# Mamba mixer of a one-core encoder step: step sizes with tokens on partitions, sample state products four at a time, and additions split around a convolution

## What is computed

```
def mamba2_mixer(u, conv_buf, ssm_state, w_in, conv_w, conv_b, dt_bias, A_log, Dp, norm_g, w_out):
    zxbcdt = u @ w_in
    ...
    xbc, new_buf = causal_conv(xbc, conv_buf, conv_w, conv_b)
    xbc = jax.nn.silu(xbc)
    ...
    dt = jax.nn.softplus(dt_raw.astype(jnp.float32) + dt_bias.astype(jnp.float32))
    A = -jnp.exp(A_log.astype(jnp.float32))
    y, s_new = ssd_scan(xs, dt, A, Bm, Cm, ssm_state)
    ...
    y = rmsnorm(y * jax.nn.silu(z), norm_g)
    return y @ w_out, new_buf, s_new
```

## Time and profile before

| | us |
|---|---|
| median of 3 runs | 1870.8 (1869.88 to 1873.21) |
| the profiled execution | 1868.97 |
| its span | 1867.2 |
| TensorE busy in it | 1822.4 (98%) |
| DVE busy | 1139.9 (61%) |
| ACT busy | 825.5 (44%) |
| POOL busy | 253.0 (14%) |

### The profile page before, as it was taken

How to read it: one execution, slowest core, us unless ns; L and a number is a source line. 1 busy time by engine, 2 the same in 40 slices (tenths; PEclk the granted TensorE clock), 3 DMA queues, 4 the chain that set the end, 5 groups by cost and what they waited for, 6 DMA issues and landing times.

```text
span 1867.2 us, 28243 instructions
## 1 busy us (share of the span) xinstructions
PE 1822.4 (98%) x10554; PEld 1735.5 (93%) x10554; DVE 1139.9 (61%) x1697; ACT 825.5 (44%) x1421; POOL 253.0 (14%) x299
## 2 busy tenths in 40 slices
PE   8999999999999999999999999999998999999997
PEld 8999999798888999999999999986777899999997
DVE  6545447888789754544775454456777756545444
ACT  5333325564574433333563333346665544333232
POOL 1000110313214000011400001122112130000110
PEclk9999999999999999999999999999999999999999
DMA  6444444465452534444444434441124534344441
GB/s 208 124 124 132 139 136 147 143 214 190 160 192 85 189 117 131 127 144 136 117 142 122 134 119 142 138 161 39 46 84 140 163 114 138 118 135 124 141 141 57
DMA packets 67652, 249.71 MB, mean 134 GB/s; under 512 B 8328, under 2 KB 9608, under 8 KB 66288
## 3 DMA queue, kind: packets, MB, share of 16 engines
q1 hardware_dynamic: 57584, 205.32, 36.0%
q0 software_dynamic: 9984, 43.24, 7.1%
HBM read 235.74 MB, written 12.12 MB: 133 GB/s over the span
## 4 chain that ended last, share of the span: by engine, by line
PE 79%; DVE 12%; ACT 4%; issue 2%; DMA 2%; POOL 1%; SPq 0%; DVEq 0%; POOLq 0%; ACTq 0%
PE pair L1854 23%; PE pair L1856 22%; PE pair L1855 22%; DVE wlo L1226 2%; PE pair L2273 1%; PE pair L2274 1%; PE pair L2275 1%; DVE cy L1354 1%; DMA lowA<-in_cacheT 1%; PE pair L2364 1%; ACT seg L842 1%; PE pair L2055 1%; DMA wv<-in_wv 1%; DVE xl L1236 1%; DVE S L1450 1%
## 5 line engine op out<-in xcount | busy, mean ns | idle before, releaser
L1854 PE MATMUL pair<-xh,whi 128*128 128x384 f32 x1928 | 651.3, 338 | 6.0 <-DVE xl L1236 4.9
L1856 PE MATMUL pair<-xh,wlo 128*128 128x384 f32 x1928 | 645.6, 335 | 0.0
L1855 PE MATMUL pair<-xl,whi 128*128 128x384 f32 x1928 | 645.5, 335 | 0.0
L1226 DVE TENSOR_TENSOR wlo<-raw,whi 128x1024 fp32r<-128x1024 f32 (+3 forms) x372 | 465.7, 1254 | 174.8 <-ACT whi L713 165.7
L713 ACT ACTIVATE whi<-raw 128x1024 fp32r<-128x1024 f32 (+2 forms) x369 | 378.6, 1029 | 283.1 <-PE pair L1856 269.9
L1854 PEld LDWEIGHTS pair<-xh,whi 128*128 128x128 f32 x1928 | 362.9, 188 | 15.0 <-issue 9.1
L1855 PEld LDWEIGHTS pair<-xl,whi 128*128 128x128 f32 x1928 | 362.9, 188 | 1.7 <-issue 1.0
L1856 PEld LDWEIGHTS pair<-xh,wlo 128*128 128x128 f32 x1928 | 362.7, 188 | 0.0
L1246 DVE TENSOR_TENSOR tg<-pair,rstd 128x384 f32<-128x384 f32 x88 | 49.1, 558 | 328.0 <-PE pair L1856 327.3
L1854 PE MATMUL pair<-ah,whi 128*128 128x384 f32 x704 | 236.6, 336 | 0.0
L1856 PE MATMUL pair<-ah,wlo 128*128 128x384 f32 x704 | 236.5, 336 | 0.0
(11 more groups left out here) (397 smaller groups left out, 2273.4 us busy)
## 6 DMA issues: line engine op xcount, KB each, us to landing
raw<-in_stream SPq DMA_DIRECT2D x372, 512.0 KB, 3.6
S<-in_ssm POOLq DMA_DIRECT2D x4, 2048.0 KB, 9.3
out_ssm_s<-S POOLq DMA_DIRECT2D x4, 2048.0 KB, 8.1
seg<-acs_rows POOLq DMA_DIRECT2D x12, 512.0 KB, 6.1
cTb<-in_cacheT POOLq DMA_DIRECT2D x10, 512.0 KB, 3.9
kn<-rs_rows SPq DMA_DIRECT2D x16, 264.0 KB
lowC<-in_cache SPq DMA_DIRECT2D x8, 512.0 KB, 3.3
lowA<-in_cacheT POOLq DMA_DIRECT2D x6, 512.0 KB, 5.9
```

The costliest lines, as they stand in the source:

```text
L1226: V.tensor_tensor(wlo[:, r, 0:w], raw[:, r, 0:w], whi[:, r, 0:w].bitcast(F32), ALU.subtract).then_inc(lo_ready, 1)
L1854: M(out, whi[:, r, ws], mh_(k), start=first and k == k0, stop=False)
L1855: M(out, whi[:, r, ws], ml_(k), start=False, stop=False)
L1856: ins = M(out, wlo[:, r, ws], mh_(k), start=False, stop=last and k == k1 - 1)
```

## The change

Step sizes: `in_proj(0, 0)` and `(0, 1)` are now ahead of most of the step-size work. DVE scales the raw values once (32x384), TensorE turns them right after `in_proj(0, 1)` (three transposes in place of six), and the rest of softplus runs on 128x96 tiles with tokens on partitions, spread between the first convolutions. ACT loads the tables for Exp and Ln, and later Silu, ahead of need, and runs `decay_exps` before its part of `in_proj(0, 5)`. `decay_sums` goes from behind `in_proj(0, 5)` to behind `in_proj(0, 4)`.

Sample states: four products at a time in four row tiles and four PSUM banks, two quartets in a group, one between `y_tile` 1 and 2, one behind `in_proj(g + 1, 1)`. `out_proj(g, 0)` and `(g, 1)` each go behind one more in_proj block. DVE's third and fourth state_add stand before and behind the convolution of `in_proj(g + 1, 1)`, and the evacuation and convolution of `in_proj(g + 1, 2)` now precede f_add of output block 0.

End of the mixer: the sums of squares become six products with one column; Sqrt and reciprocal work on 128x3, and a product of ones with a diagonal spreads the result over partitions. DVE does all of the residual. Second layer: `q_evac(9..11)` behind `key_square(0)`, the reciprocal of past_rstd behind `absorbed(7)`, `rs_turn` behind the scores of unit 1 and its copies behind `keys_split(1)`.

```diff
-        order += [("in", g, 0), ("in", g, 1), ("out", g - 1, 0), ("in", g, 2), ("out", g - 1, 1), ("in", g, 3), ("in", g, 4)]
+        order += [("in", g, 0), ("in", g, 1), ("in", g, 2), ("out", g - 1, 0), ("in", g, 3), ("out", g - 1, 1), ("in", g, 4)]
...
-            dts = sb("dts", [HEADS, 2], F32, ssd)
+            dts = sb("dts", [P, 2, HEADS], F32, ssd)
...
         def state_bank(g, i):
-            r = i // 2
-            if g == GROUPS - 1:
-                return bank[(4, 5, 6, 7, 4, 7, 5, 6)[i]]
-            return bank[3 * (i % 2) if r == 3 else 4 + i % 2]
+            return bank[(6, 7, 4, 5, 4, 7, 5, 6)[i] if g == GROUPS - 1 else (6, 7, 4, 5, 4, 5, 0, 3)[i]]
...
             def dt_exps():
+                act.preload_act_table(ACT.Exp)
                 act.wait_ge(dt_dve, 1)
-                step(A(dv[2], dv[1], ACT.Abs))
-                A(dts[:, 1:2], dts[:, 1:2], ACT.Exp)
-                A(dv[3], dv[2], ACT.Exp, scale=-1.0).then_inc(dt_act, 1)
+                A(dts[:, 1, :], dts[:, 1, :], ACT.Exp)
+                step(A(dv[1], dv[0], ACT.Abs))
+                A(dv[2], dv[1], ACT.Exp, scale=-1.0).then_inc(dt_act, 1)
+                act.preload_act_table(ACT.Ln)
...
+                if g == 0:
+                    decay_exps()
+                    act.preload_act_table(ACT.Silu)
                 in_proj(g, 5)
                 if g == 0:
                     silu(0, 5)
-                    decay_exps()
...
-            for e in range(9, 12):
-                q_evac(e)
...
             key_square(0)
+            for e in range(9, 12):
+                q_evac(e)
...
                 if i == 2:
                     dve.wait_ge(dt_act, 1)
-                    V.tensor_scalar(dv[4], dv[3], 1.0, None, ALU.add).then_inc(dt_dve, 1)
+                    V.tensor_scalar(dv[3], dv[2], 1.0, None, ALU.add).then_inc(dt_dve, 1)
                     dve.wait_ge(dt_dve, 2)
-                    step(V.reciprocal(dv[6], dv[4]))
...
+                    step(V.reciprocal(dv[4], dv[3]))
...
             for g in range(GROUPS):
                 last = g == GROUPS - 1
                 if g:
                     in_proj(g, 0)
-                    in_proj(g, 1)
+                    evac(g, 1)
+                    state_add(g - 1, 2)
+                    conv(g, 1)
                     state_add(g - 1, 3)
+                in_proj(g, 2)
+                if g == 0:
+                    dt_step(3)
+                if g:
                     out_proj(g - 1, 0)
-                in_proj(g, 2)
+                in_proj(g, 3)
                 if g:
                     out_proj(g - 1, 1)
-                in_proj(g, 3)
-                if g == 0:
-                    dt_step(4)
                 in_proj(g, 4)
...
                 state_add(g, 0)
                 state_add(g, 1)
                 y_rows(g)
-                if not last:
-                    state_add(g, 2)
...
-            V.reciprocal(rstd[:, 0, :], std[:, :]).then_inc(y_rstd, 1)
+            step(V.reciprocal(rows[:, 0, :], rows[:, 0, :]))
+            V.tensor_tensor(std[:, :].rearrange("p (t l) -> p t l", t=TT), bc(ident[:, :], (P, TT, P), 1),
+                            bc(rows[:, 0, :], (P, TT, P), 2), ALU.mult).then_inc(y_rstd, 1)
...
-            dve.wait_ge(past_std, 2)
-            V.reciprocal(ksq[:, :, 6:8], ksq[:, :, 6:8]).then_inc(past_rstd, 1)
             keys_split(0)
...
             absorbed(6)
             absorbed(7)
+            dve.wait_ge(past_std, 2)
+            V.reciprocal(ksq[:, :, 6:8], ksq[:, :, 6:8]).then_inc(past_rstd, 1)
...
+            def sample_states(g, e):
+                if e == 0:
+                    pe.wait_ge(in_evac, 10 * g + 10)
                     pe.wait_ge(yo_ready, 2 * g + 2)
                     pe.wait_ge(s1_ready, 2 * g + 2)
...
+                else:
                     pe.wait_ge(state_ready, 8 * g + 4)
+                    if g < GROUPS - 1:
+                        pe.wait_ge(y_evac, 4 * g + 4)
+                    else:
+                        pe.wait_ge(y_std, 2)
+                for j in range(4):
                     rows32 = slice(32 * j, 32 * j + 32)
-                    ins = M(state_bank(g, i)[:, :], Bm[rows32, e, :], xw[rows32, 2, :], start=True, stop=True)
+                    ins = M(state_bank(g, 4 * e + j)[:, :], Bm[rows32, e, :], xw[rows32, 2, :], start=True, stop=True)
                 ins.then_inc(state_ps, 1)
...
-            M(bank[5][:, 0:TOK], ones[:, :], sqacc[:, 0, :], start=True, stop=False)
             pe.wait_ge(y_sq, 4 * GROUPS)
-            M(bank[5][:, 0:TOK], ones[:, :], zs[:, 3, :], start=False, stop=True).then_inc(y_sum_ps, 1)
+            for t in range(TT):
+                M(bank[5][:, t:t + 1], sqacc[:, 0, tiles(t)], ones[:, 0:1], start=True, stop=False)
+                ins = M(bank[5][:, t:t + 1], zs[:, 3, tiles(t)], ones[:, 0:1], start=False, stop=True)
+            ins.then_inc(y_sum_ps, 1)
             out_proj(GROUPS - 1, 0)
-            pe.wait_ge(y_std, 1)
-            sample_states(GROUPS - 1, 3)
+            pe.wait_ge(y_rstd, 1)
+            M(bank[5][:, 0:TOK], ones[:, :], std[:, :], start=True, stop=True).then_inc(y_sum_ps, 1)
+            pe.wait_ge(y_std, 2)
+            sample_states(GROUPS - 1, 1)
...
-            pe.wait_ge(past_rstd, 4)
-            rs_turn(bank[2], 6, 8)
...
+                if u == 0:
+                    pe.wait_ge(past_rstd, 4)
+                    rs_turn(bank[1], 6, 8)
+                if u == 3:
+                    pe.wait_ge(rs_ev, 3)
```

More of the change, by code:

```diff
@@ L165, in build @@
         am = Bm[:, :, :].rearrange("p a b -> p (a b)").rearrange("p (s h) -> p s h", s=STREAMS)
-        dv = [seg[0:HEADS, i // 2, (i % 2) * TOK:(i % 2 + 1) * TOK] for i in range(4)] + \
-             [xdt[0:HEADS, i, 0:TOK] for i in range(3)]
+        dt_heads = xdt[0:HEADS, 0, 0:TOK]
+        dv = [seg[:, 0, 96 * i:96 * i + 96].rearrange("p (t h) -> p t h", t=TT) for i in range(7)]
         with ExitStack() as ple:
@@ L814, in in_proj @@
                       ACT.Copy).then_inc(cout_ready, 1)
[L815 removed]
+                if 1 <= b <= 6 and (g or 1 < b < 6):
                     silu(g, b - 1)
@@ L896, in _ @@
                         seg_exp(g, t)
+                if g == 0:
+                    seg_diff(g, 0)
+                    seg_exp(g, 0)
                 in_proj(g, 7)
+                if g == 0:
+                    seg_diff(g, 1)
+                    seg_exp(g, 1)
                 in_proj(g, 8)
-                if g == 0:
-                    for t in range(2):
-                        seg_diff(g, t)
-                        seg_exp(g, t)
-                in_proj(g, 9)
                 if g == 0:
@@ L906, in _ @@
                     seg_exp(g, 2)
+                in_proj(g, 9)
                 for i in range(4):
@@ L924, in _ @@
             act.wait_ge(y_sum_ps, 1)
-            A(std[:, :], bank[5][:, 0:TOK], ACT.Sqrt, bias=EPS, scale=1.0 / D_INNER).then_inc(y_std, 1)
+            A(rows[:, 0, :], bank[5][:, 0:TT], ACT.Sqrt, bias=EPS, scale=1.0 / D_INNER).then_inc(y_std, 1)
             hi_split(n + 3)
+            act.wait_ge(y_sum_ps, 2)
+            A(rstd[:, 0, :], bank[5][:, 0:TOK], ACT.Copy).then_inc(y_std, 1)
             for b in range(3):
@@ L1180, in _ @@
             keys_split(1)
+            act.wait_ge(rs_turn_ps, 3)
+            act.wait_ge(rs_st, 16 * 3)
+            A(rsT[0:2 * MH, :], bank[1][0:2 * MH, 0:3 * P], ACT.Copy)
+            A(rsT2[0:2 * MH, 0:P], bank[1][0:2 * MH, 3 * P:4 * P], ACT.Copy).then_inc(rs_ev, 1)
             for u in range(UNITS):
@@ L2079, in _ @@
                 in_proj(g, 0)
+                in_proj(g, 1)
+                if g == 0:
+                    dt_turn()
                 if g:
-                    sample_states(g - 1, 2)
-                in_proj(g, 1)
-                if g:
-                    sample_states(g - 1, 3)
-                    out_proj(g - 1, 0)
+                    sample_states(g - 1, 1)
                 in_proj(g, 2)
                 if g:
+                    out_proj(g - 1, 0)
+                in_proj(g, 3)
+                if g:
                     out_proj(g - 1, 1)
-                in_proj(g, 3)
                 in_proj(g, 4)
                 if g == 0:
-                    dt_turn()
+                    decay_sums()
                 elif not last:
@@ L2095, in _ @@
                 in_proj(g, 5)
-                if g == 0:
-                    decay_sums()
-                elif not last:
+                if g and not last:
                     out_proj(g - 1, 3)
```

123 lines of the change are left out of this document (44 added, 79 removed).

## The result

The changed kernel ("after") takes 1875.1 us, the kernel before 1872.0 (medians of 20 runs each): 3.2 us slower, ratio 1.0020 with an interval of 1.0012 to 1.0028. The forecast was 4.0 us faster, and the time lies above its range. TensorE has less to do (1820.9 us against 1822.4 busy, though slow stretches count in both) and idles more.

The account below looks back on a forecast made before the run. TensorE, busy nearly all the span, was taken as the bound, with DVE level between groups. Terms -3.0, -1.0, -0.5, -0.3, +0.15, +0.9 and -0.25 made -4.0 us: 1866.8 us, range 1860.0 to 1872.0.

Parts of the forecast that it names:

- The step sizes: Before the turns of group 0: shorter DVE chain and earlier decay_sums bring the turns 3.0 us sooner, ends -4.0 and -1.3.
- Rival C: Sample states: four row tiles do not run together, a quartet takes 2.12 us; -0.8 us in all, 1870.0; chance 0.06.
- quartets and order without the sharing: Between groups 1 and 2: if POOL's sums did not lengthen DVE's work, the turns would move by -2.4 us.
- Sharing of DVE and POOL: Between groups 1 and 2: POOL's sums lengthen DVE's split and convolution ahead of f_add by 1.9 us, leaving -0.5.
- Between 0 and 1: Groups 0 to 1: three POOL sums lengthen DVE's work by 1.4 us, leaving -1.0 us, ends -2.4 and 0.
- together 0: TensorE's clock: the fall behind the mixer goes, -1.7 us, and one before the turns of group 0 comes, +1.7.
- Groups 2 to 3: Turns wait for SiLU of B and C, following DVE and ACT, so only -0.3 us shows, ends -1.4 and +0.4.
- The end of the mixer: With the second layer's start: new waits nearly cancel two pairs saved, +0.15 us, ends -0.8 and +1.5.
- The sample attention: Moved reciprocal of past_rstd delays the scores, +0.9 us; sign, the 1.75 us wait growing to 2.6; rs_turn fits a wait.
- A: All the quartets' saving lands, POOL's sums miss the path and both clock falls stay away: -9.0 us, 1861.8; chance 0.20.
- B: Between groups, PSUM evacuation on DVE takes all the quartets' saving; other terms leave -2.0 us, 1868.8; chance 0.18.
- D: Clock falls behind every new wait and the fall at 612 stays, five of 1.7 us: +4.5 us, 1875.3; chance 0.09.

Follow-up runs that it names:

- e1: The changed kernel with POOL's sums of squares of groups 0 to 2 held until f_add of output block 0 is done; 1864.1 us, ratio 0.9948.
- e3: The changed kernel with useless products of ones filling four long TensorE waits (turns of group 0, output block 1 of groups 0 to 2); 1872.9 us, ratio 0.9996.
- e4: The kernel before with only the step sizes of the change (tokens on partitions, early table loads, decay_sums moved); 1870.8 us, ratio 0.9982.
- e7: The kernel before with POOL's sums of squares of groups 0 to 2 held until f_add of output block 1; 1873.7 us, ratio 0.9998.
- e8: The kernel before with only the sample attention moves (reciprocal of past_rstd, rs_turn and its copies); 1876.7 us, ratio 1.0027.
- e9: e8 with POOL's two stores of the turned values, and their wait, put behind the loads of stream 2; 1873.7 us, ratio 1.0010.
- after_again: The changed kernel, unchanged, run and profiled a second time; 1875.6 us, ratio 1.0011.
- e5: e1 with the sample attention moves undone, as in the kernel before; 1859.6 us, ratio 0.9921.
- e10: The changed kernel with only the sample attention moves undone; 1873.9 us, ratio 1.0007.
- e6: e5 with 14 useless products of ones in TensorE's wait before the turns of group 0; 1857.7 us, ratio 0.9917.

## Why the prediction was wrong, step by step

**Right.** The quartet costs what a pair did, 1.07 for the 1.06 taken; y_rows begin 1.4 us sooner once the 2.0 us gained earlier are taken off (1.39 forecast), the turns of group 0 come behind one wait of 3.4 (forecast 3) and decay_sums without one, and the slow stretch behind the mixer is gone. The step sizes gave 2.4 at the turns, inside the ends of −4.0 and −1.3 but short of the 3.0 taken. Their slow stretch then came as counted, cost 1.25 where 1.7 was taken, and left 1.15. Rival C falls with the quartet's row. What the step worked out for quartets and order without the sharing, −2.4 between groups 1 and 2, is borne out by e1: 73.2 us from turns to turns where before has 75.9, −2.7.

**Sharing of DVE and POOL, the term that decides: 1.9 us taken, 3.3 measured.** The step "1.73 against 1.22 and 3.39 against 2.00, 1.9 us together" took the lengthening from a place where the sums began beside f_add and an evacuation. The earlier trace rows had it: the sums run from 452.36 to 457.86, but the evacuation at 453.40 has its usual 0.42 us, so part of the sums passed beside work that they don't lengthen. In after the split and the taps lie almost wholly beside sums, 2.55 + 4.00 against 3.22 us: twice their time. f_add between groups 1 and 2 ends at 456.95; with the 2.0 us gained before it that is 1.5 later than the 457.5 forecast, about the difference of 1.4. Between 0 and 1 three sums cost 2.56 + 3.39, that is 2.7 us where 1.4 was taken, and −0.3 came out for −1.0.

In all these rows a DVE instruction with both inputs in SBUF takes up to about twice its time beside POOL's sums, and one that reads PSUM (evacuation 0.42, in before and in e1) its usual time. The Trainium skill, SBUF — State Buffer, Who interferes with whom, says this: with two SBUF inputs a DVE instruction contends with a GpSimd instruction that reads SBUF; with at most one, and outside its two-port modes, it does not. The traces here agree (4.00 against 2.00, and 0.42 in both places). Read by the sources of their operands, would have shown which part of the 5.5 us was shared, and that the new place has none of the unshared kind.

**The clock: "together 0" was wrong.** One fall was counted at the turns and came. Two more came at `out_proj(1, 1)` and `out_proj(2, 1)`, where the waits were 3.5 us each; 2.6 was forecast for the first, and for the second the step had none. Together with the sharing they make the +2.2 and +2.0 in place of −0.5 and −0.3. For 1 to 2: −0.5, +1.4 for the sharing and 1.6 for the fall (e3) make +2.5, where +2.2 was measured. The wait of 2.9 at `out_proj(0, 1)` was followed by no fall. That a fall is "near an even chance for a wait of 2 to 3 us" was read from one execution. Over more of them it goes by the place: behind the 2.2 us wait at the end of before's mixer the clock fell in each of five profiles (before, e4, e7, e8, e9), behind the 2.1 us wait before the turns of group 3 in one of the same five (e4).

**Groups 2 to 3: "the turns wait for SiLU … not TensorE's blocks".** The turns of group 3 still wait for ACT, only 1.2 us instead of 2.1 (4.6 less 3.4 in the waits above), so they were not the cover that the step took them for: SiLU there follows DVE, and DVE is late by the same sums, for which the step had no term here. With the sums away (e1) the stage is 2.9 us shorter than in before, with them 2.0 longer.

**The end of the mixer.** The fall that was counted as gone at 1.7 us is gone, and the stage gained nothing: TensorE then waits 1.4 us for DVE's square sum before the next norm. The step had followed the chain to the 2.2 us wait and not beyond it. Whether these tail waits (1.6, 1.6, 1.4) can be had was not tried.

**The sample attention: +0.9 taken, +2.2 and +3.0 measured.** The reciprocal costs about what was said, 0.7 us at the scores and 0.8 at the end of e9's stretch, but the sign that was named for it, a wait of 2.6 us there, did not come: the wait is 2.0 where it was 1.75, since `rs_turn` now fills 0.4 of it. The step that failed is "rs_turn behind the scores fits into a wait". It priced the turn on TensorE, and not the copies on ACT and the stores that POOL issues for it, behind which stood the loads of the next stream. In after the visible loss is the slow clock, though: TensorE's waits in its stretch sum to 8.1 us, no more than before's 8.5, and its work to 77.9 instead of 75.4. A slow stretch was there in each of the six profiles with the moves (after, after_again, e1, e3, e8, e9) and in two of the six without (e4, e5), whose stretches took 84.2 and 85.0 us all the same; so the moves make one likelier, but e9's came behind a wait that before has as well.

**The rivals.** A's condition ("POOL's sums miss the path") is what e1 makes true, and its mechanism is right: with the sums out of the path, the turns of group 3 start 9.0 us ahead of before in e5 (543.6 against 552.6), and the times of e5 show 13.8. That the first is A's number for the whole is chance, since the fall at the turns, which A had away, is there. A did not come true in the kernel as it was changed. B does not hold: in e1 the same evacuations and state_adds run on DVE, and no wait for f_add is left. The agreement with the trace that was noted beside it was with a working, not with a row. The rule that was cited beside it, from the Trainium skill, TensorEngine Tiling (Array Packing), Performance Considerations, is then not what bound here: PSUM's evacuation was not the limit, DVE's time lost to POOL was. D gave the time, 1875.3, but only a part of the mechanism: of the places it added, one had a fall (`out_proj(1, 1)`), and `out_proj(0, 1)`, output block 2, the y norm's end and 612 had none; one that it did not name had (`out_proj(2, 1)`). That its number fits is luck: the rest of the loss came from the sharing and from POOL's queue. Its "three waits of 1.75 us and more without a fall" said nothing about waits of 3.5.

## What to carry to other kernels

When work is moved ahead of an instruction that another engine waits for, lay POOL's instructions beside it again: look at what DVE runs in exactly that stretch, with the source of both operands, and price those with two SBUF inputs at about twice their time. A step that is moved takes its DMA issues along, and a queue's next load waits behind them: list who stands behind each wait in the new order. And a wait of some microseconds on TensorE costs more than its length when a slow stretch of the clock follows, so a saving that ends in a wait there is worth less than the row of waits says.

## What was not expected of the hardware

Beside POOL's sums DVE ran at half its rate, 1.22 to 2.55 and 2.00 to 4.00 us, and POOL pays too: its four sums took 5.50 and 5.61 us where they met split and taps, and 4.29 in e7. DVE work that reads PSUM kept its time beside them (0.42). TensorE's clock fell to 1.2 GHz in every one of six profiles with the unfilled wait of 3.4 us before the turns of group 0 (after, after_again, e1, e4, e5, e10: 0.50 to 0.57 in 327.8 to 331), and behind both unfilled 3.5 us waits for f_add in all three profiles that have them (after, after_again, e10), but in none of these three behind the 2.9 us wait at `out_proj(0, 1)`. It fell behind the 2.2 us wait at the end of before's mixer in all five profiles that have it. Behind waits of 1 to 2 us before the turns of group 0 in before, in the sample attention and at 1240 it fell in some executions of the same work and not in others. Products that do nothing, put into such a wait, kept it at 2.4 GHz each time (e3, e6).
